# Narrower first products in the triangular inverse of the delta rule, with a zeroed buffer for each level

## The reference, cut to what matters

```
def rwkv7_scan(r, w, k, v, kk, a):
    def step(state, inp):
        r_t, w_t, k_t, v_t, kk_t, a_t = inp
        sa = jnp.einsum('bhvk,bhk->bhv', state, -kk_t)
        state = (state * w_t[:, :, None, :]
                 + sa[..., None] * (kk_t * a_t)[:, :, None, :]
                 + v_t[..., None] * k_t[:, :, None, :])
        return state, jnp.einsum('bhvk,bhk->bhv', state, r_t)
```

## Time and profile before

| | |
|---|---|
| Median of three runs | 3403.94 us (3391.94 to 3407.72) |
| Profiled execution, device time | 3404.24 us |
| Its span | 3402.2 us |
| TensorE matmul busy | 3302.5 us, 97% |
| VectorE, ScalarE, GpSimd busy | 1750.2, 1192.7 and 410.2 us |
| TensorE's granted clock, mean | 0.982 of full speed |

### The profile page before, as it was taken

The page is one execution under the profiler, slowest core; times in us unless marked ns, Lnnn a source line. Parts: engine busy times, 40 slices in busy tenths (PEclk is TensorE's granted clock), DMA queues, the critical chain, the costliest instruction groups (busy, mean ns, idle before and its releaser), DMA issues.

```text
span 3402.2 us, 44422 instructions
## 1 busy us (share of the span) xinstructions
PE 3302.5 (97%) x18534; PEld 2622.3 (77%) x18534; DVE 1750.2 (51%) x2533; ACT 1192.7 (35%) x1884; POOL 410.2 (12%) x318
## 2 busy tenths in 40 slices
PE   8999999899999999999999999999999999999999
PEld 6766778676677888887777778888888887678887
DVE  7854454744446744336767554433565334454433
ACT  3344433434443522224323342222353224342221
POOL 0000011000001311012322211100101011011110
PEclk9999999899999999999989999999999999899999
DMA  6721122221122332333200013232323322022332
GB/s 231 224 95 62 50 99 93 74 81 62 56 81 69 117 100 93 99 95 119 69 14 2 27 44 120 95 99 88 104 82 98 99 91 89 10 66 94 99 99 81
DMA packets 83911, 295.47 MB, mean 87 GB/s; under 512 B 9472, under 2 KB 12800, under 8 KB 81664
## 3 DMA queue, kind: packets, MB, share of 16 engines
q1 hardware_dynamic: 78384, 270.61, 24.5%
q10 hardware_dynamic: 5328, 22.02, 1.9%
HBM read 283.94 MB, written 8.65 MB: 86 GB/s over the span
## 4 chain that ended last, share of the span: by engine, by line
PE 84%; DVE 7%; ACT 2%; issue 2%; POOL 1%; DMA 0%; DVEq 0%; POOLq 0%; ACTq 0%
PE acc L479 67%; PE acc L1513 1%; DVE w_lo L390 1%; PE acc L2492 1%; PE acc L3266 1%; PE aux L3230 1%; PE aux L1794 1%; ACT w_hi L383 1%; PE acc L1825 1%; PE acc L2496 1%; DVE ssd_ex L1415 1%; PE acc L2482 1%; PE aux L2449 1%; PE aux L3235 1%; PE aux L1812 1%
## 5 line engine op out<-in xcount | busy, mean ns | idle before, releaser
L479 PE MATMUL acc<-op_hi,w_hi 128*128 128x512 f32 x2624 | 1086.5, 414 | 26.6 <-ACT conv_sums L1206 11.8
L383 ACT ACTIVATE w_hi<-raw 128x1024 fp32r<-128x1024 f32 (+2 forms) x476 | 494.5, 1039 | 1535.9 <-PE acc L479 1500.7
L479 PE MATMUL acc<-op_hi,w_lo 128*128 128x512 f32 x2624 | 1030.0, 393 | 0.0
L479 PE MATMUL acc<-op_lo,w_hi 128*128 128x512 f32 x2624 | 1029.4, 392 | 0.0
L390 DVE TENSOR_TENSOR w_lo<-raw,w_hi 128x1024 fp32r<-128x1024 f32 (+2 forms) x476 | 577.0, 1212 | 291.9 <-ACT w_hi L383 291.5
L479 PEld LDWEIGHTS acc<-op_hi,w_hi 128*128 128x128 f32 x2624 | 496.1, 189 | 187.5 <-issue 85.6
L479 PEld LDWEIGHTS acc<-op_hi,w_lo 128*128 128x128 f32 x2624 | 496.1, 189 | 108.2
L479 PEld LDWEIGHTS acc<-op_lo,w_hi 128*128 128x128 f32 x2624 | 497.4, 190 | 102.5 <-issue 10.1
L479 PE MATMUL acc<-ffn_hi,w_hi 128*128 128x512 f32 x800 | 311.4, 389 | 0.0
L479 PE MATMUL acc<-ffn_hi,w_lo 128*128 128x512 f32 x800 | 311.2, 389 | 0.0
L479 PE MATMUL acc<-ffn_lo,w_hi 128*128 128x512 f32 x800 | 311.2, 389 | 0.0
(11 more groups left out here) (585 smaller groups left out, 3900.6 us busy)
## 6 DMA issues: line engine op xcount, KB each, us to landing
raw<-in_w SPq DMA_DIRECT2D x436, 512.0 KB, 3.5
late_ada<-in_ada ACTq DMA_DIRECT2D x32, 512.0 KB, 4.2
raw<-in_w SPq DMA_DIRECT2D x32, 384.0 KB, 3.0
ada<-in_ada ACTq DMA_DIRECT2D x4, 1024.0 KB, 14.1
ada<-in_ada SPq DMA_DIRECT2D x4, 1024.0 KB, 21.5
x_mid<-x SPq DMA_DIRECT2D x16, 256.0 KB, 3.3
x<-x_mid SPq DMA_DIRECT2D x2, 2048.0 KB, 7.8
skew<-rel_rows SPq DMA_DIRECT2D x12, 192.0 KB, 3.1
```

Of the source, the lines that this page charges most:

```text
L383: act.activation(self.w_hi[g % AHEAD][:, 0:k, :], self.raw[s][:, 0:k, :], ACT.Copy).then_inc(self.split_hi.handle, 1)
L479: mm = pe.matmul(self.bank(s, g), w[:, k, :], a[:, k, 0:s.n], start=(k == 0 and q == 0), stop=(k == k_tiles - 1 and q == 2))
```

## The change

The first products of levels 1 to 5 take as values only the second half of each group of columns, 32 instead of 64, and write to the same places of PSUM as before, so that the unused half stays unwritten. ScalarE copies only those 128x128 values, to a buffer of the level and of e, instead of one 128x256 block to G. The other half of each of these ten buffers is set to zero once by GpSimd and stays zero. The buffers of levels 1 to 4 are a new array `inv_grown` (8 KB in each partition), those of level 5 lie at two gaps of the memory plan, for which `ln_factor` moves. The new clearings stand between the first and the second that were there. ScalarE's first copy gets one more wait, for the clearing.

```
+        last = [core.place(f"inv_last{e}", [P, T // 2], kb)[:, :] for e, kb in enumerate((15, 89))]
+        self.grown = [[core.inv_grown[:, 2 * level + e, :] for e in range(2)] for level in range(self.LEVELS - 2)] + [last]
+        self.grown_zeroed = core.share("inv_grown_zeroed", 1)
-        self.ln_factor = core.place("ln_factor", [P, 2 * NT], 89.0)
+        self.ln_factor = core.place("ln_factor", [P, 2 * NT], 88.3125)
...
-                            mm = pe.matmul(block(first_banks[e], n, i), block(C[e], n, i), diagonal(X[e], n, i),
-                                           start=True, stop=True)
+                            mm = pe.matmul(self.columns_of(block(first_banks[e], n, i), level, 1), block(C[e], n, i),
+                                           self.columns_of(diagonal(X[e], n, i), level, 1), start=True, stop=True)
...
-                    bank = next_banks[e]
+                    bank, grown = next_banks[e], self.grown[level - 1][e]
...
-                                           self.columns_of(block(G[e], n, i), level, 1), start=True, stop=True)
+                                           self.columns_of(block(grown, n, i), level, 1), start=True, stop=True)
...
-                            mm = pe.matmul(self.packed(bank, level, 1, rows[i], n), block(G[e], n, i),
+                            mm = pe.matmul(self.packed(bank, level, 1, rows[i], n), block(grown, n, i),
...
                     if m == 0 and level == 1 and e == 0:
+                        act.wait_ge(*self.grown_zeroed.ge(1))
                         act.wait_ge(*self.turned.ge(4))
-                    act.activation(G[e][rows, :], first_banks[e][rows, :], ACT.Copy
-                                   ).then_inc(*self.copied.inc())
+                    if level < self.LEVELS:
+                        dst = self.columns_of(self.grown[level - 1][e], level, 1)
+                        src = self.columns_of(first_banks[e], level, 1)
+                    else:
+                        dst, src = G[e][0:HD, :], first_banks[e][0:HD, :]
+                    act.activation(dst, src, ACT.Copy).then_inc(*self.copied.inc())
...
             pool.memset(core.x[:, 2:8, :], 0.0).then_inc(*self.zeroed.inc())
+            pool.memset(core.inv_grown[:, :, :], 0.0)
+            for e in range(2):
+                zero = pool.memset(self.grown[-1][e], 0.0)
+            zero.then_inc(*self.grown_zeroed.inc())
             pool.memset(core.squares[:, 2:4, :], 0.0).then_inc(*self.zeroed.inc())
...
+        core.inv_grown = core.sb("inv_grown", [P, 2 * (Rwkv.LEVELS - 2), T // 2])
```

More of the change, by code:

```diff
@@ L2647, in inverse @@
             for level in range(1, self.LEVELS + 1):
-                rows = slice(0, P if level < self.LEVELS else HD)
                 for e in range(2):
```

## The result

| | before | after |
|---|---|---|
| Median, 20 runs each | 3403.66 us (3391.94 to 3412.77) | 3414.22 us (3400.45 to 3422.68) |
| Ratio, 95% interval | | 1.0034 [1.0024, 1.0044] |
| Profiled execution, its span | 3404.24, 3402.2 us | 3412.43, 3410.4 us |
| Granted clock, mean over the span | 0.982 | 0.978 |

The change makes the kernel 10.6 us slower, 0.3%. The forecast was 3404 us with a range up to 3414: the time lies just outside. It is within the half per cent to which the prediction gave 87%, but with 20 runs on either side the interval is 0.1% wide to each side, and the loss is plain.

What follows compares the result with a forecast made beforehand. TensorE's own list of small products was taken to set the pace in the delta rule. First products -1.5, copies -0.8 and clearings +2.3 summed to 0.0 us, so 3404 us was forecast, range 3394 to 3414.

Steps and rivals of the forecast that it cites:

- the half per cent: Whole kernel: time stays within 0.5%, 17 us, of before; chance 87%.
- Clearings: GpSimd at the stage's start: new clearings delay the fourth tile without cover, costing 2.3 us; ends 0 and 2.4.
- First products: Levels 1 to 5: halved columns save 0.025 us in each of 60 groups, 1.5 us; ends 0 and 1.8.
- Copies: ScalarE's sixty halved copies, 0.107 us shorter each, save 0.8 us where TensorE waited; ends 0 and 6.4.
- the two bounds: Gain from copies: 1.2 us by eleven held weight loads, 0.3 us by three idle matmuls.
- The rule of PSUM's lines: First products' writes: non-contiguous access slows matmuls significantly, so they would get slower; the rule gives no figure.
- The rival with gaps: First products: writes with gaps slow each group by 0.48 us, 29 us over 60, giving 3434 us; chance 5%.
- the term of the clock: Behind the gap before the fourth tile: difference taken as 0; ends 0.5 us less and 1.6 us more.
- the rival that the clock falls more often: Four steady periods: each gains a slow stretch of 7 us, giving 3432 us; chance 4%.
- The prediction's own sign of being wrong: Delta rule: among the signs of being wrong, a granted clock below 1.00 between 1740 and 1916 us.
- not within 2: Sign of being right: the delta rule's end lies within 2 us of where it was.

Runs made afterwards that it cites:

- e1: Before plus only the new buffers, their three clearings and the wait for them; products and copies unchanged. Ratio 1.0018, 3355.4 us at equal clock.
- e4: After with first products of 64 columns again and the new clearings moved later, leaving half copies and new buffers. Ratio 0.9999, median 3401.78 us.
- e3: After with first products of 64 columns again; clearings in place, half copies kept. Ratio 1.0015, median 3405.41 us.
- e2: After with its new clearings moved behind the differences that the fourth tile needs; products stay at 32 columns. Ratio 1.0037, median 3410.44 us.
- e5: Before with GpSimd's old clearings planned 12 us later, behind the first differences. Ratio 0.9978, median 3394.75 us.
- e6: e5 plus half copies and the new buffers, cleared at start + 21.5; first products of 64 columns. Ratio 0.9987, median 3394.50 us.
- e14: e4 with first products of 48 columns in pair 1 only. Ratio 1.0024, median 3408.40 us.
- e16: e4 unchanged, run once more for a second profile; no second stretch at 1.2 GHz in pair 1.
- e7: e4 with first products of 32 columns in pair 1 only. Ratio 1.0032, median 3412.76 us.
- e8: e4 with first products of 32 columns in all pairs except pair 1. Ratio 1.0014, median 3402.24 us.
- e9: After with each first product of 32 columns in pair 1 issued twice, same result. Ratio 1.0048, median 3414.36 us.
- the fill: e5 with six unused products added where TensorE waits between 1717 and 1740 us. Ratio 0.9991, median 3396.92 us.
- e13: e4 with pair 1's first products passing all 64 columns in the stepped order of the narrow form. Ratio 1.0014, median 3401.58 us.

## Why the prediction was wrong

**Right: the sum without the clock.** The sum was 0.0 us; at equal clock after is 3353.7 +- 0.3, before 3353.1 +- 0.1, so +0.6. The nearness is in part luck: the copies gave no gain where 0.8 was forecast, and the first products perhaps more than theirs. Term by term:

- *Clearings*, +2.3: the trace shows 2.25, e1 gives 2.3 +- 0.3. Taking them off the path again gives back 1.8 +- 0.7 (e4 against e3), but only 0.3 +- 0.9 in e2 against after. That they had no cover was right, and e5 shows that the whole wait there could go.
- *First products*, -1.5: the steady period became 0.17 us shorter for 10 groups, 0.017 us each and 1.0 us over 60; e3 gives 2.0 +- 0.7, e2 against e4 0.5 +- 1.0. Inside the ends of 0 and 1.8 but for that error.
- *Copies*, -0.8: mis-sized. Three pairs of kernels (e3 against e1, e6 against e5, e4 against before) give +0.3, +0.1 and +0.8 us, each +- 0.4 to 0.6. The held weight loads shrank from 7.1 to 6.0 us, about the forecast 11 x 0.107, and no gain shows in the runs. Of the two bounds the smaller one, 0.3 us from the idle matmuls, was the nearer: those waits shrank from 1.8 to 1.5 us. That a held weight load costs nothing by itself is my reading; no run tests it alone.
- *The rule of PSUM's lines* (the Trainium skill, PSUM — Partial Sum Buffer, section Specifications (TRN2)): not borne out here. Groups that write in runs of 2 to 16 fp32 with gaps take 0.47 us against 0.49 with adjacent columns, and the periods became shorter. (At level 5 the 32 columns of a product are adjacent, so that level is no test.) The rival with gaps falls.

**Wrong: the term of the clock.** In the sum I took 0 for it and looked at one place alone, behind the gap before the fourth tile. For the rest there was the rival that the clock falls more often, and the failing step stands in it: "it decides from three of them", and as reason against "the periods have idle time of only 4%, and the clock is 1.00 in all four". Two faults. The four periods were taken as alike, all or none, though pair 1 follows directly on a stretch at 1.2 GHz and the others do not; one stretch more in pair 1, by my own price 7 us, was in no case and in no end of the range. And a small idle share of the period was taken for what protects the clock. The runs show otherwise: with the same busy time and the same wait of 1.2 us ahead (e14 and e16) the clock fell with 48 columns and stayed with 64, and with 32 it fell in four profiles of four. The mean of 4% also hid that wait, behind which five of the six falls came; it is longest in pair 1 (1.19 us in before, 0.77 us at its place in pair 2). The rival had the mechanism and the sign, with 4%; what came in the profile of after is one quarter of its case. The prediction's own sign of being wrong, a clock below 1.00 between 1740 and 1916, is what came (0.70 from 1740 to 1784), and the delta rule ended 15.2 us late, not within 2.

**What it cost.** In the profile pair 1 takes 8.4 us longer. Over the runs, after has 145 us at the lower level and before 113; 32 us x 0.41 = 13 us, and 0.6 at equal clock, beside a difference of 13.7 us between the mean of after (3413.0) and that of the 96 runs of before (3399.3); against the 20 runs of before beside it, which lay higher (mean 3403.1), it is 9.9. e7 reproduces the loss from narrow products in pair 1 alone (3411.9 us in the mean; e4 without them 3399.9).

**What stays open.** Over the profiles the second stretch lasts 22 us in the mean of the four with 32 columns in pair 1 and 2 us in the mean of the ten with 64: some 20 of those 32 us. The first stretch, which ends in pair 1, is 23.9 us long in each of those four, 20.5 in e14, and 17.1 to 20.5 (mean 19.1) in those ten: some 5 more. The later stretches of e8 and e9 belong to the rest, but with so few profiles its size can't be told from chance. Nor is it shown why the fill keeps the clock up in its place and gains nothing in the mean. That it is the columns and not the form of the access rests on e7, e14 and e13; by what measure the chip judges them no run shows, nor why the same kernel has the stretch once and not the next time (e4 and e16).

## What to carry to other kernels

Where small products follow one another, a cut in their columns saves little time (here 4% of a group for half of the columns) and can cost TensorE's clock, even though the engine's busy share stays the same; look first at the places that lie just behind a stretch at the lower clock or behind a wait of TensorE, and price one more such stretch in the range. Compare the mean granted clock of many runs, not that of one profile, and take its part off before a term of 1 or 2 us is judged. Clearings belong behind whatever the next tile waits for: moving the old ones by 12 us in the planned order gained 0.2% [0.1, 0.3], while first products and copies together were reckoned at 2.3 us, 0.07%.

## What the runs showed that I had not expected

- The clock fell to 1.2 GHz behind 10 us in which TensorE was busy for 9.42, and a wait of 1.2 us (e14, 48 columns), and did not fall behind the same in e16 (64 columns). Once low it stayed low for some 20 us with TensorE busy throughout (22.00 of 22 us at a clock of 0.59 in e4). With 64 columns in pair 1 the clock there was 1.00 in nine of ten profiles.
- A run's time follows its mean clock: 0.41 us for each us at 1.2 GHz over 237 runs. Before scatters by 20 us from run to run, and nearly all of that is the clock; without it the mean of 96 runs is known to 0.1 us.
- The same program at the same place can have the stretch or not (e4 and e16), so one profile of before without it is no safe ground.
- Halving a copy from 0.384 to 0.278 us sixty times changed nothing that 12 runs can tell.
